# A two-layer hybrid decoder trunk: products of the token mixers merged, sample rows weighed with 128 rows, and one mixer's clamp moved to the eviction

## The reference

```python
z = x @ w_in                                   # 1024 -> 15*512 + 8, split into the heads of four mixers
hA, C1, n1, m1 = _mlstm_chunked(q, k, v, ig, lf, C0, n0, m0)     # A: 4 heads of 128
hB, Sr1 = _retention_chunked(rope(q), rope(k), v, log_gamma, S)  # B: 4 heads
kc = (1 - lb) * sigmoid(-f_c)                                    # C: 4 heads
log_f = log1p(-minimum(kc, GATE_CLAMP))
hC, Sh1 = _gla_chunked(silu(q_c), kc, i_c, log_f, S)
yD = bg * short_conv(cg * x_d, buf, conv_w)                      # D
mix = sum over branches of sigmoid(x @ w_gate + b) * (branch @ w_branch)
h   = LN(alpha * x + mix @ w_out)
out = LN(alpha * h + relu(h @ w_up)**2 @ w_down)
```

## Time and profile before

| | |
|---|---|
| median of 3 runs | 1595.56 us (1595.1 to 1599.61) |
| profiled execution | 1595.64 us, span of its instructions 1593.8 us |
| mean granted TensorE clock | 0.987 |
| PE matmuls | 10442 records, of them 8688 dense |
| busy share DVE, ACT, POOL | 63%, 42%, 56% |
| DMA | 223.61 MB, mean 140 GB/s |
| chain that ended last | PE 87%, DVE 7%, ACT 3%, POOL 1% |

### The profile page before, as it was taken

How to read it: one execution, slowest core, us unless ns; L and a number is a source line. 1 busy time by engine, 2 the same in 40 slices (tenths; PEclk the granted TensorE clock), 3 DMA queues, 4 the chain that set the end, 5 groups by cost and what they waited for, 6 DMA issues and landing times.

```text
span 1593.8 us, 26238 instructions
## 1 busy us (share of the span) xinstructions
PE 1538.8 (97%) x10442; PEld 1477.8 (93%) x10442; DVE 996.3 (63%) x1929; ACT 666.0 (42%) x1220; POOL 888.1 (56%) x381
## 2 busy tenths in 40 slices
PE   7899999999999999999888999999999999999996
PEld 7899998999999999999888999889999999999996
DVE  4874775237676777754447747752467767777544
ACT  5434443333444544433344444434344445444333
POOL 6456444444445666677654554444444556666674
PEclk9999999999999999999999999999999999999998
DMA  8333353443354444444433334433334444444442
GB/s 284 119 115 123 137 177 101 154 135 122 121 175 151 142 138 148 151 148 151 139 106 106 119 120 164 161 124 132 122 135 141 156 140 141 136 151 150 149 151 79
DMA packets 66257, 223.61 MB, mean 140 GB/s; under 512 B 8024, under 2 KB 12632, under 8 KB 66136
## 3 DMA queue, kind: packets, MB, share of 16 engines
q1 hardware_dynamic: 66136, 221.93, 43.3%
HBM read 206.33 MB, written 15.58 MB: 139 GB/s over the span
## 4 chain that ended last, share of the span: by engine, by line
PE 87%; DVE 7%; ACT 3%; issue 1%; POOL 1%; DMA 0%; DVEq 0%; ACTq 0%
PE gps L1284 25%; PE gps L1286 24%; PE gps L1285 24%; PE xp L1523 2%; PE xp L1525 1%; PE xp L1460 1%; DVE mix L981 1%; PE xp L1438 1%; PE xp L1419 1%; PE xp L1512 1%; PE xp L1429 1%; PE xp L1421 1%; POOL wlo L594 1%; PE xp L1408 1%; ACT whi L615 1%
## 5 line engine op out<-in xcount | busy, mean ns | idle before, releaser
L594 POOL TENSOR_TENSOR wlo<-raw,whi 128x1024 fp32r<-128x1024 f32 x362 | 875.7, 2421 | 687.2 <-ACT whi L615 413.2
L1284 PE MATMUL gps<-xh,whi 128*128 128x320 f32 (+1 forms) x2000 | 643.3, 322 | 29.7 <-DVE zc L854 12.0
L1285 PE MATMUL gps<-xl,whi 128*128 128x320 f32 (+1 forms) x2000 | 625.7, 313 | 0.0
L1286 PE MATMUL gps<-xh,wlo 128*128 128x320 f32 (+1 forms) x2000 | 624.9, 312 | 0.0
L615 ACT ACTIVATE whi<-raw 128x1024 fp32r<-128x1024 f32 x258 | 272.3, 1056 | 348.7 <-PE gps L1286 297.7
L1284 PEld LDWEIGHTS gps<-xh,whi 128*128 128x128 f32 x2000 | 381.3, 191 | 38.5 <-POOL wlo L594 19.3
L1285 PEld LDWEIGHTS gps<-xl,whi 128*128 128x128 f32 x2000 | 382.8, 191 | 3.4 <-issue 0.4
L1286 PEld LDWEIGHTS gps<-xh,wlo 128*128 128x128 f32 x2000 | 382.3, 191 | 0.0
L1284 PE MATMUL gps<-ah,whi 128*128 128x320 f32 x640 | 199.1, 311 | 0.6
L1286 PE MATMUL gps<-ah,wlo 128*128 128x320 f32 x640 | 197.8, 309 | 0.0
L1285 PE MATMUL gps<-al,whi 128*128 128x320 f32 x640 | 197.7, 309 | 0.0
(11 more groups left out here) (299 smaller groups left out, 1893.3 us busy)
## 6 DMA issues: line engine op xcount, KB each, us to landing
raw<-in_w SPq DMA_DIRECT2D x362, 512.0 KB, 3.5
s<-in_st SPq DMA_DIRECT2D x24, 512.0 KB, 4.3
out_ss<-s SPq DMA_DIRECT2D x24, 512.0 KB, 2.7
con<-in_cst SPq DMA_DIRECT2D x4, 526.0 KB, 5.9
out_sp<-pst SPq DMA_DIRECT2D x24, 64.0 KB, 2.6
mix<-in_x SPq DMA_DIRECT2D x4, 320.0 KB, 4.9
out_y<-mix SPq DMA_DIRECT2D x8, 160.0 KB, 1.9
ee<-in_cst SPq DMA_DIRECT2D x1, 224.0 KB, 4.4
```

The lines of the kernel that those rows point to most:

```text
L594: nc.gpsimd.tensor_tensor(wlo[:, c % RING, :, :], raw[:, c % RING, :, :], whi[:, c % RING, :, :].bitcast(F32), ALU.subtract).then_inc(lo_d ...
L1284: M(out, hi, xhi, start=start, stop=False)
L1285: M(out, hi, xlo, start=False, stop=False)
L1286: return M(out, lo, xhi, start=False, stop=stop)
```

## The change

- **State reads.** The two groups of four state reads go to the same columns of `xp[4]`, the second adding to the first. So that each sample's 8 queries meet only their own rows, `qw` has 32 columns for each sample, zero but for the first 8, and the second group's window starts 8 columns early. `seen` is half as wide, and `add_states` is one product of 64 columns instead of two of 32.
- **Normaliser of the new state.** The weights of the last column (`ee`) are copied as a 129th column of `vw`, so line 1515's two products go into line 1512's.
- **Rows.** `row` and `wi` become `cap` (448 columns, in the arrangement of the scores) and `top` (384 columns), so three products and two products become one each. DVE's part of `a_row` has one addition, one copy and one negation more.
- **128-row weighing.** The third tile of `va` and `vc` is zeroed by POOL at the start and again at the layer change (rows 64 to 127 stay zero), and `weigh` uses 128 rows for it; ACT's value copies wait for the zeroing (`pad_zero`).
- **Clamp.** ACT writes fC's exponential into the PSUM bank instead of `tt`; DVE reads it twice, for k and for the clamped k. `c_log` begins with ACT; the block's first value is subtracted at its end for two heads at once, and `c_first` begins with ACT.

Left out of the diff: declarations, `queries()` and `per_seq()` in the places that write `qw`, and comments.

```diff
 PHASES = {
-    "c_log": (("dve", BEFORE), ("act", 0), ("dve", 1)),
-    "c_first": (("dve", BEFORE), ("act", 0), ("dve", 1)),
+    "c_log": (("act", BEFORE), ("dve", 0)),
+    "c_first": (("act", BEFORE), ("dve", 0)),
...
-            nc.gpsimd.memset(qw[:, :, NS:], 0.0)
+            nc.gpsimd.memset(qw[:, :, :], 0.0)
             nc.gpsimd.memset(iff[:, :, :], 0.0).then_inc(setup_pool, 1)
+
+            def zero_pads():
+
+                nc.gpsimd.memset(vc[:, :, 2, :], 0.0).then_inc(pad_zero, 1)
+                nc.gpsimd.memset(va[:, :, 2, :], 0.0).then_inc(pad_zero, 1)
+
+            zero_pads()
...
                 if c >= RING and ends_norm((c - RING) % NSLOT) == 1:
                     shift(2 * ((c - RING) // NSLOT) + 1)
+                    pool.wait_ge(slot_done, c - c % NSLOT)
+                    zero_pads()
...
                 if kind == "vt":
+                    act.wait_ge(pad_zero, 2 * (layer + 1))
...
+                elif a == "fC":
+                    nc.scalar.activation(gps[g % BANKS][:, 0:T], t, ACT.Exp, scale=-1.0).then_inc(act_part, 1)
                 else:
-                    nc.scalar.activation(t, t, ACT.Exp, scale=-1.0 if a == "fC" else 1.0).then_inc(act_part, 1)
+                    nc.scalar.activation(t, t, ACT.Exp).then_inc(act_part, 1)
...
-                    done(nc.scalar.activation(seen[:, :, :], xp[4][:, 0:2 * P].rearrange("p (r c) -> p r c", r=2), ACT.Copy))
+                    done(nc.scalar.activation(seen[:, :], xp[4][:, 0:P], ACT.Copy))
...
                 if a == "fC":
-                    V.tensor_scalar(zc[:, 1, b, :], t, oml[:, layer, b:b + 1], None, ALU.mult).then_inc(tile_free["dve"], 1)
+                    ps = gps[g % BANKS][:, 0:T]
+                    V.tensor_scalar(zc[:, 1, b, :], ps, oml[:, layer, b:b + 1], None, ALU.mult)
+                    V.tensor_scalar(z12[:, 0, b, :], ps, oml[:, layer, b:b + 1], CLAMP, ALU.mult,
+                                    ALU.min).then_inc(tile_free["dve"], 1)
...
-                if stage == "c_log" and k == 0:
-                    done(V.tensor_scalar(z12[:, 0, 2 * h:2 * h + 2, :], zc[:, 1, 2 * h:2 * h + 2, :], CLAMP, None, ALU.min))
-                elif stage == "c_log":
+                if stage == "c_log":
 
                     for hd in (2 * h, 2 * h + 1):
                         last = V.tensor_tensor_scan(zc[:, 2, hd, :], c_("scan"), z12[:, 0, hd, :], 0.0, ALU.mult, ALU.add)
-                    done(last)
-                elif stage == "c_first" and k == 0:
-                    b = zc[:, 2, h, :].rearrange("p (b m) -> p b m", m=4)
-                    z = z12[:, 0, h, :].rearrange("p (b m) -> p b m", m=4)
-                    done(V.tensor_tensor(z, b, b[:, :, 0:1].to_broadcast([P, T // 4, 4]), ALU.subtract))
+                    link(last)
+                    b = zc[:, 2, 2 * h:2 * h + 2, :].rearrange("p h (b m) -> p h b m", m=4)
+                    z = z12[:, 0, 2 * h:2 * h + 2, :].rearrange("p h (b m) -> p h b m", m=4)
+                    done(V.tensor_tensor(z, b, b[:, :, :, 0:1].to_broadcast([P, 2, T // 4, 4]), ALU.subtract))
...
-                    link(V.tensor_tensor(row[:, 0, :], row[:, 1, :], xp[3][0:H, 0:T], ALU.add))
+                    V.tensor_tensor(top[:, 0:SEQ], cap[:, 0:SEQ], xp[3][0:H, 0:SEQ], ALU.add)
+                    link(V.tensor_tensor(top[:, SEQ:T], cap[:, 384:SP4], xp[3][0:H, SEQ:T], ALU.add))
...
+                    link(V.tensor_scalar(cap[:, 256:384], cap[:, P:256], -1.0, None, ALU.mult))
+                    V.tensor_scalar(cap[:, 0:256], cap[:, 0:256], -1.0, None, ALU.mult)
+                    done(V.tensor_scalar(cap[:, 384:SP4], cap[:, 384:SP4], -1.0, None, ALU.mult))
...
+                    if n == "A":
+                        V.tensor_copy(vw[:, :, P], ee[:, 255:384:128])
...
-                return M(bank[:, SEQ:T], lhs(2), pt[0:NS, h, 384:SP4], start=False, stop=False, skip_group_check=True)
+                return M(bank[:, SEQ:T], lhs(2), pt[:, h, 384:SP4], start=False, stop=False, skip_group_check=True)
...
-                        q = qw[:, h, b * DS:b * DS + 32]
-                        last = M(xp[4][32 * i:32 * (i + 1), r * P:(r + 1) * P], q, s0[:, j % 2, b, :], start=True, stop=True,
+                        q = qw[:, h, 32 * b - r * DS:32 * (b + 1) - r * DS]
+                        last = M(xp[4][32 * i:32 * (i + 1), 0:P], q, s0[:, j % 2, b, :], start=r == 0, stop=r == 1,
                                  tile_position=(0, 32 * i), skip_group_check=True)
...
-                pick = ident.rearrange("p (i t) -> p i t", t=32)[:, :, 0:DS]
-                for r in range(2):
-                    out = xp[3][:, SEQ + 32 * r:SEQ + 32 * (r + 1)].rearrange("p (i t) -> p i t", t=DS)
-                    last = M(out, seen[:, r, :], pick, start=False, stop=r == 1, skip_group_check=True)
-                return last
+                pick = ident.rearrange("p (i r t) -> p r i t", i=4, t=DS)[:, 0:2, :, :]
+                out = xp[3][:, SEQ:T].rearrange("p (r i t) -> p r i t", r=2, t=DS)
+                return M(out, seen[:, :], pick, start=False, stop=True, skip_group_check=True)
...
-                    for j, (col, src) in enumerate(((slice(0, 256), slice(0, 256)), (slice(256, 384), slice(P, SEQ)),
-                                                    (slice(384, SP4), slice(SEQ, T)))):
-                        M(xp[0][:, col], sel, row[:, 1, src], start=j == 0, stop=False, skip_group_check=True)
+                    M(xp[0][:, 0:SP4], sel, cap[:, :], start=True, stop=False, skip_group_check=True)
...
-                    M(xp[2][:, 0:T], sel, row[:, 0, :], start=True, stop=False, skip_group_check=True)
-                    done(M(xp[2][:, T:384], sel, wi[:, :], start=False, stop=True, skip_group_check=True))
+                    done(M(xp[2][:, 0:384], sel, top[:, :], start=True, stop=True, skip_group_check=True))
...
-                    weigh(xp[3], lambda i: v_of(n, h, i), h)
+                    weigh(xp[3], lambda i: (va if n == "A" else vc)[:, h, i, :], h)
...
-                        weigh(xp[4], lambda i: ones[0:TILES[i][1], 0, :], h)
+                        weigh(xp[4], lambda i: ones[:, 0, :], h)
...
-                        v = v_of(n, h, i) if n == "C" else vw[:, i, :]
-                        M(xp[0][:, 0:P], kt[:, i, :], v, start=i == 0, stop=False, skip_group_check=True)
+                        width = P + 1 if n == "A" else P
+                        v = v_of(n, h, i) if n == "C" else vw[:, i, 0:width]
+                        M(xp[0][:, 0:width], kt[:, i, :], v, start=i == 0, stop=False, skip_group_check=True)
                     if n == "A":
-                        for i in range(2):
-                            M(xp[0][:, P:P + 1], kt[:, i, :], ee[:, (255, 383)[i]:(256, 384)[i]], start=False, stop=False,
-                              skip_group_check=True)
```

More of the change, by code:

```diff
@@ L382, in trunk @@
             vf = sb("vf", [P, 2, T], F32, early)
+            iff_fm = vf[0:2 * H, 0, :]
         ah = sb("ah", [P, KF, T], F32R)
@@ L395, in trunk @@
         kt = sb("kt", [P, 3, P])
-        vw = sb("vw", [P, 2, P])
+        vw = sb("vw", [P, 2, P + 1])
         pst = sb("pst", [P, 2, P])
@@ L401, in trunk @@
         tt = sb("tt", [P, BANKS, T])
-        qw = sb("qw", [P, H, NS + 32 - DS])
+        qw = sb("qw", [P, H, 32 * NB])
         qn = sb("qn", [P, NS])
-        seen = sb("seen", [P, 2, P])
+        seen = sb("seen", [P, P])
         dec = sb("dec", [P, H, NB])
@@ L412, in trunk @@
         bif = sb("bif", [2 * H, DEPTH])
-        iff_fm = sb("iff_fm", [2 * H, T])
         n0s = sb("n0s", [P, DEPTH, H, NB])
@@ L416, in trunk @@
         m0s = sb("m0s", [H, DEPTH, NB])
-        row = sb("row", [H, 2, T])
-        wi = sb("wi", [H, NS])
+        cap = sb("cap", [H, SP4])
+        top = sb("top", [H, 384])
         mou = sb("mou", [H, 1 + NB])
@@ L446, in trunk @@
         x_hi, x_lo = sem("x_hi"), sem("x_lo")
+        pad_zero = sem("pad_zero")
         dve_chain, act_chain = sem("dve_chain"), sem("act_chain")
@@ L478, in per_seq, with queries, sample_tokens @@
             return ap.rearrange("p (b t) -> p b t", t=DS)
+        def queries():
+            return qw[:, :, :].rearrange("p h (b c) -> p h b c", c=32)[:, :, :, 0:DS]
+        def sample_tokens(ap):
+            return ap[:, :, SEQ:T].rearrange("p h (b t) -> p h b t", t=DS)
         def sample_u(h):
@@ L689, in phase @@
                     nc.scalar.activation(z12[:, 1, :, :], z12[:, 1, :, :], ACT.Exp)
-                    nc.scalar.activation(qw[:, :, 0:NS], zc[:, 2, :, SEQ:T], ACT.Exp)
+                    nc.scalar.activation(queries(), sample_tokens(zc[:, 2, :, :]), ACT.Exp)
                     done(nc.scalar.activation(dec[:, :, :], zc[:, 2, :, SEQ + DS - 1:T:DS], ACT.Exp))
@@ L696, in phase @@
                 elif stage == "a_exp":
-                    nc.scalar.activation(row[:, 0, :], row[:, 0, :], ACT.Exp, scale=-1.0)
```

(15 more changed lines are left out.)

18 lines of the change are left out of this document (9 added, 9 removed).

## The result

The changed kernel takes 1574.04 us (median of four runs, 1573.05 to 1576.17) where the kernel before takes 1595.33 beside it: a ratio of 0.986 with a 95% interval of 0.984 to 0.988. The profiled execution took 1573.41 us, its span is 1571.6. The forecast was 1570 with a range of 1563 to 1579. Of the 25.6 us of its sum, 22.2 came in the profiled execution and 21.3 in the medians.

What follows compares the result with a forecast made beforehand. TensorE (PE), busy 97% of the span, was taken as the bound. 12.6 + 1.0 + 2.3 + 10.2 - 0.5 = 25.6 us off about 1595.6 gave 1570 us, range 1563 to 1579.

Steps and rivals of the forecast that it cites:

- C's stretch: Where mixer C's tiles are evicted: clamp at eviction, subtraction moved from c_first to c_log; 1.3 us per c_first slot, 10.2 us taken.
- Weighing and state reads: In the heads' `num`: 128-row weighing 7.7 us, summed state reads 5.5 us, 0.6 us back for `seen`; 12.6 us left.
- a wait for `seen` in all heads: Sign that the forecast is wrong: PE waiting for ACT's copy in every head; four heads waited already.
- The wait between the two reads of one bank: In the state reads summed in PSUM: possible wait of at most 3.6 us, taken as 0.
- Rows in one piece: In A heads: six passes become two and four more become two; 0.13 us per head, 1.0 us for eight.
- Normaliser: In A heads, line 1515's passes join the values' product: 0.34 us in each of eight, 0.4 us back, net 2.3 us.
- rival 3: C stretch gives back its gain (fC evictions hold PE's banks, or line 983 caught again): 1575 to 1580; 0.24 shared with another rival.
- Pads: POOL's memsets at the layer change delay its subtraction by 1 us: 0.5 us lost, bounds -0.6 and 1.2.
- favourable end: Layer change: if memsets don't hold DVE operations with two SBUF inputs, the sum is 1 us larger.
- Rival 4 and 5: 4: low clock behind heads with less PE work, 1637 us, chance 0.03; 5: dropped products save nothing, 1590 to 1597, chance 0.04.
- 3 us either way: Whole kernel: where the granted clock falls may shift, adding 3 us in either direction.

Runs made afterwards that it cites:

- e1_rows64: The changed kernel with only the third product of each weighing put back to 64 rows (32 weighings): 1578.9 us, ratio 0.989 to the kernel before.
- e5_weigh128: The kernel before with only the zero pads, their semaphore and the 128-row weighing added: 1591.6 us, ratio 0.9964.
- e4_seen_first: The changed kernel with ACT copying `seen` ahead of the eviction of the tile just ended, in C and A heads: 1571.6 us, ratio 0.9835.
- e6_products_only: The changed kernel with mixer C's stretch (clamp, scans, subtractions, exponential) as in the kernel before, all merged products kept: 1582.5 us, ratio 0.9904.
- e3_one_multiply: The changed kernel with the two 128x320 multiplies of c_first joined in one of 128x640: 1567.75 us, ratio 0.9815.
- e8_after_again: The changed kernel itself, unaltered, run once more beside other runs: 1576.3 us, ratio 0.9855.
- the kernel with both edits: The changed kernel with c_first's two multiplies joined and ACT's copy `seen` ahead of the eviction in C and A heads: 1563.2 us, ratio 0.978.

## Why the prediction was right, point by point

**The time** was 4 us above the forecast and inside the range. The profiled execution misses 3.4 us from the 25.6. Against it stand 2.5 us in C's stretch, 1.0 of a wait in C's last heads that the sum didn't have, 0.4 in the weighing and 1.2 of longer low clock at the start, which is chance. For it stands less low clock elsewhere, some 1.5 us of it in A's `fin`. The terms came out as follows.

**Weighing and state reads (12.6 us).** The 24 `num` are 12.2 us shorter in the trace (79.7 to 67.4 us). The mechanism is right in the main, and the term is mis-sized in two ways that nearly cancel, which is luck. Unhindered, a head gives 0.56 us and not 0.47. But `seen` takes back more than the 0.6 us of the forecast, which counted only the four heads that already waited. It named "a wait for `seen` in all heads" as a sign of being wrong; in 16 of 24 nothing is left to spare, in eight PE waits. The four C heads of layer 0 gained 0.51, 0.25, 0.31 and 0.52, two of layer 1 lost 0.2 and 0.7 behind the late weight. What was missed is that a wait of zero in the earlier trace rows says nothing of how near the next one is: the distance from the end of `seen` to `add_states`, 0.24 us, would have told. The wait between the two reads of one bank, taken as 0, is 0: the groups of reads start 0.11 and 0.09 us apart as before. `e1_rows64` and `e5_weigh128` show the padding's share, `e4_seen_first` shows `seen`.

**Rows in one piece (1.0 us)**: 0.13 us a head, as forecast. **Normaliser (2.3 us)**: 0.34 us in an A head's `fin` as forecast. The waits before `fin`'s first product grew from 4.5 to 6.0 us, but only 0.3 of this lies in A heads, within the 0.4 set aside. Another 1.0 us lies in the last C head of the two layers (of the two waits of 0.15 there before, that view counts one), here layer 0's before and after:

```profile
209.81 0.57 PE L1512 MATMUL xp<-vc,kt 128*128 128x128 f32 x3 [0.15 <-issue]
```

```profile
206.26 0.57 PE L1535 MATMUL xp<-vc,kt 128*128 128x128 f32 x3 [0.67 <-issue]
```

No copy was added there. The wait is 0.32 us with the padding alone, so it comes with the shorter `num` ahead of it: once more a wait that less work on PE lengthens, and 1.0 us that no term of the sum held. What PE waits for there isn't shown. The products together, `e6_products_only`, gave 15.3 us where the sum had 15.4.

**C's stretch (10.2 us)**: 7.7 in the trace. The cycle came out as worked out (4.2 us for 4.3), and so did the scans (held; PE's gap behind the second c_log shrank by 0.4 us in layer 0 and 0.8 in layer 1). What failed is the last slot of the four: the forecast gave each the same 1.3 us, but the slot behind the last has its cast from ACT, ready early, so POOL runs on without a pause. That is rival 3's mechanism, "line 983 is caught by the next subtraction as well", for 983's successor 984 (L1005 now) and in one slot of four, and `e3_one_multiply` shows it. The fC evictions, rival 3's other half, hold PE for 0.4 us in all.

**Pads (-0.5 us)**: 0.0 in the profiled execution, 1.1 to 1.2 us lost in those of `e8_after_again` and `e5_weigh128`. At the layer change DVE and POOL now stand so:

```profile
785.91 0.54 DVE L1253 SCALAR_TENSOR_TENSOR xl<-mix,prm,xh 128x320 fp32r<-128x320 f32 x1
786.37 0.54 DVE L1244 SCALAR_TENSOR_TENSOR mix<-mix,prm,rs 128x320 f32<-128x320 f32 x1
786.83 2.65 DVE L1253 SCALAR_TENSOR_TENSOR xl<-mix,prm,xh 128x320 fp32r<-128x320 f32 x1
```

```profile
785.58 0.52 POOL L593 MEMSET vc<- 128x512 f32 x1
786.04 0.52 POOL L594 MEMSET va<- 128x512 f32 x1
786.53 2.60 POOL L612 TENSOR_TENSOR wlo<-raw,whi 128x1024 fp32r<-128x1024 f32 x1
```

The memsets let the first low part through in 0.54 us where the earlier trace rows have 2.63: PE starts 2.1 us sooner. The second low part is then caught instead, with one more wait of 1.0 us and low clock, and the 2.1 us are gone again, or more where the low clock lasts longer. That the memset doesn't hold DVE agrees with the Trainium skill, "SBUF — State Buffer", section "SBUF: two separate sides". That the whole term would then be at its favourable end, as the prediction went on, doesn't come out.

**Rival 4 and 5.** Low clock behind every head didn't come: besides the start, the layer change and the end the changed kernel falls to it six times, the kernel before seven. Dropped products were saved. But the clock explains what the steps don't. By the sum used above it cost 11.4 us in the kernel before and 3.8 in `e1_rows64`, whose profiled span is the lower for it. In the changed kernel 1.2 us went at the very start, where the low clock ended at 13.8 us instead of 11.1. One execution differs from another of the same kernel by 1 to 3 us in this way, the "3 us either way" of the forecast.

## What to carry to other kernels

When work is taken out of the engine that bounds a kernel, list for each of its waits how early the other side is today, not only how long it is waited for: 0.3 us less work used up the slack of 0.19 us that a copy had, and where the copy itself was late it became a wait. When an operation that another engine holds back is removed, look at what moves into its place, and at the last repetition apart from the others, for its successor may come from another queue. Two short operations behind one another can be held twice by an engine that goes from one long operation straight to the next, where one of double length was held once. And add up the low clock before pricing an edit by its time: here it differed by 3 us between two executions of one kernel, and by 8 between those of two kernels a few us apart.

## What the hardware showed that was not expected

- A copy from SBUF to SBUF of 128x320 (f32) beside a GpSimd subtraction took 2.31 us, and 0.31 beside none; a scan 2.81 and 0.79; a multiply of 128x640 beside one took 2.85.
- An operation that had started wasn't held by the next subtraction: the multiply of 128x640 ran on to 79.14 us though GpSimd's next subtraction began at 78.42.
- Two passes of 64 columns and 128 rows between products of 128 rows take 0.17 us up to the next product's start, 0.06 for the first of them; the same columns with 64 rows take 0.36 in the same place, 0.16 for the first.
- Where TensorE's granted clock falls to 1.2 GHz isn't settled by the stall ahead of it: behind the wait of 1.9 us on one of qC's evictions it fell in one execution of the kernel with both edits (at 58.6 us) and not in the other, and not in the kernel before, whose wait there is 2.4 us.
